# Moving two weight splits from the smallest to the largest attention tiles, and cutting the key-compression rows in two

## What is computed

```python
h = x @ w_in_even[li]
qa, ka, va, qn, kc, vc, ksl, vsl, kw, vw, g = _split(h, EVEN_SPLITS)
o_a = diff_attention(qa, ka, va, diff_lambda[li], diff_subln[li], layer)      # 4 heads x 2 halves, causal
# nsa_attention: 8 query heads in 2 groups, three branches
blocks = t[:, cmp_idx] + pe[j]          # windows of 32 rows of kc and vc, every 16 rows
hid    = gelu(blocks @ w1[j] + b1[j]);  out = hid @ w2[j]                     # 31 compressed keys and values
o_c = softmax(q . kc) vc;  o_s = softmax(q . rope(ksl)) vsl;  o_w = softmax(q . rope(kw)) vw
o_b = g0 * o_c + g1 * o_s + g2 * o_w
mix = concat(o_a, o_b) @ w_out_even[li]
x = layer_norm(ALPHA * x + mix); ...
```

## Time and profile before

| | |
|---|---|
| median of 3 runs | 2456.62 us (2455.29 to 2457.24) |
| the profiled execution | 2456.84 us, span 2455.5 us |
| mean granted TensorE clock | 0.959 |
| busy share of the span | TensorE 93%, VectorE 42%, ScalarE 29%, GpSimd 4% |

### The profile page before, as it was taken

The page is one execution under the profiler, slowest core; times in us unless marked ns, Lnnn a source line. Parts: engine busy times, 40 slices in busy tenths (PEclk is TensorE's granted clock), DMA queues, the critical chain, the costliest instruction groups (busy, mean ns, idle before and its releaser), DMA issues.

```text
span 2455.5 us, 28478 instructions
## 1 busy us (share of the span) xinstructions
PE 2286.5 (93%) x11871; PEld 1686.7 (69%) x11871; DVE 1043.5 (42%) x1904; ACT 703.8 (29%) x1188; POOL 95.4 (4%) x96
## 2 busy tenths in 40 slices
PE   7998899979989999899788989999999999899998
PEld 6866687864434343587555778888787777788887
DVE  5347465342322233434566534233521455342335
ACT  4324354310100010223345223133223362231331
POOL 2001001010000000000000000000000000000000
PEclk9989899989999999999889999999989999999999
DMA  5232242359999999522100222323132201223230
GB/s 194 86 127 82 78 163 105 102 223 392 427 426 427 426 428 427 203 81 69 69 1 1 90 100 103 103 86 103 36 132 86 86 2 39 100 102 103 86 103 34
DMA packets 106740, 370.34 MB, mean 151 GB/s; under 512 B 15040, under 2 KB 20672, under 8 KB 94320
## 3 DMA queue, kind: packets, MB, share of 16 engines
q1 hardware_dynamic: 103584, 361.65, 39.1%
q0 software_dynamic: 3024, 6.83, 0.9%
HBM read 368.38 MB, written 4.19 MB: 152 GB/s over the span
## 4 chain that ended last, share of the span: by engine, by line
PE 78%; DMA 10%; DVE 8%; ACT 2%; issue 1%; POOL 1%; SPq 0%; DVEq 0%; ACTq 0%; POOLq 0%
PE PB L450 52%; PE PB L1898 8%; PE PB L467 5%; PE PB L460 4%; PE PB L769 4%; DMA Z<-in_w_exp_gate 4%; PE PB L661 3%; DMA FL_raw<-in_w_exp_gate 1%; DMA FH_raw<-in_w_exp_gate 1%; DMA Z<-in_w_exp_down 1%; PE PB L785 1%; DVE W L442 1%; DMA FL_raw<-in_w_exp_down 1%; PE PB L666 1%; ACT W L434 1%
## 5 line engine op out<-in xcount | busy, mean ns | idle before, releaser
L442 DVE TENSOR_TENSOR W<-R,W 128x2048 fp32r<-128x2048 f32 (+1 forms) x128 | 291.4, 2277 | 663.1 <-ACT W L434 663.0
L450 PE MATMUL PB<-W,FH 128*128 128x512 f32 (+1 forms) x1792 | 558.4, 394 | 8.1 <-DVE FL L823 6.7
L434 ACT ACTIVATE W<-R 128x2048 fp32r<-128x2048 f32 (+1 forms) x128 | 243.5, 1903 | 678.8 <-PE PB L450 671.7
L450 PEld LDWEIGHTS PB<-W,FH 128*128 128x128 f32 x1792 | 332.4, 190 | 77.4 <-DVE FL L823 8.1
L450 PE MATMUL PB<-W,hid 128*128 128x512 f32 x1536 | 349.6, 389 | 1.0 <-DVE X L2923 1.0
L450 PE MATMUL PB<-W,FL 128*128 128x512 f32 (+1 forms) x896 | 348.8, 389 | 0.0
L450 PE MATMUL PB<-FH,W 128*128 128x512 f32 (+1 forms) x1152 | 327.4, 369 | 15.6 <-ACT nsp L2878 14.3
L450 PEld LDWEIGHTS PB<-W,hid 128*128 128x128 f32 x1536 | 288.1, 188 | 61.0 <-DVE X L2923 1.4
L450 PEld LDWEIGHTS PB<-FH,W 128*128 128x128 f32 x1152 | 210.7, 191 | 52.1 <-ACT nsp L2878 14.7
L450 PE MATMUL PB<-FL,W 128*128 128x512 f32 (+1 forms) x576 | 212.2, 368 | 0.0
L450 PEld LDWEIGHTS PB<-W,FL 128*128 128x128 f32 x896 | 169.7, 189 | 35.4
(11 more groups left out here) (329 smaller groups left out, 2643.8 us busy)
## 6 DMA issues: line engine op xcount, KB each, us to landing
R<-in_mlp_w_up SPq DMA_DIRECT2D x32, 1024.0 KB, 5.3
R<-in_mlp_w_down SPq DMA_DIRECT2D x32, 1024.0 KB, 5.0
Z<-in_w_exp_down SPq DMA_DIRECT2D x14, 2048.0 KB, 30.6
Z<-in_w_exp_up SPq DMA_DIRECT2D x13, 2048.0 KB, 36.4
R<-in_w_exp_gate SPq DMA_DIRECT2D x11, 2048.0 KB, 32.3
W_raw<-in_w_exp_up SPq DMA_DIRECT2D x10, 2048.0 KB, 31.3
R<-in_w_exp_up SPq DMA_DIRECT2D x9, 2048.0 KB, 30.9
R<-in_w_in SPq DMA_DIRECT2D x12, 1024.0 KB, 5.4
```

The costliest lines, as they stand in the source:

```text
L434: k.A.e.activation(w.splits[w.split_of[u]][0][:, 0:m], w.rows(u), ACT.Copy).then_inc(*w.hi.tick(u))
L442: k.V.e.tensor_tensor(wl[:, 0:m], w.rows(u), wh[:, 0:m].bitcast(F32), ALU.subtract).then_inc(*w.lo.tick(u))
L450: ins = te.matmul(bank, l, r, start=(start and n == 0), stop=(stop and n == len(terms) - 1), skip_group_check=True)
```

## The change

Three edits. The two `cut` steps move from around `nsa[1, 1]` to the middles of `nsa[3, 0]` and `nsa[3, 1]`. The `windows` step becomes two, one for each of keys and values, with a pair between them. The copies into partitions 64 to 127 of `cs` go from VectorE to ScalarE (`act_fours`), with a bank of the transposes kept until the doubling of `ksl`, and VectorE's doubling made to wait for ScalarE's copies.

```diff
-    return ([("ks", 3)] + d3[0:2] + [("five", 0), ("five", 1), d3[2], ("five", 2), ("five", 3), d3[3], ("windows",), d2[0],
-             ("hidden", 0), d2[1], ("hidden", 1), d2[2], ("hidden", 2), d2[3], ("hidden", 3), ("dn", 3), d1[0], d1[1],
+    return ([("ks", 3)] + d3[0:2] + [("five", 0), ("five", 1), d3[2], ("five", 2), ("five", 3), d3[3], ("windows", 0), d2[0],
+             ("windows", 1), ("hidden", 0), d2[1], ("hidden", 1), d2[2], ("hidden", 2), d2[3], ("hidden", 3), ("dn", 3), d1[0], d1[1],
              ("biased",), d1[2], ("small",), d1[3], ("kc",), d0[0], d0[1], ("dn", 2), d0[2], d0[3], ("few", 3)]
-            + nsa[3, 0] + [("dn", 1), ("few", 2)] + nsa[3, 1] + [("dn", 0)] + nsa[2, 0] + [("few", 1)] + nsa[2, 1]
-            + nsa[1, 0] + [("few", 0), ("cut", 0)] + nsa[1, 1] + [("cut", 1)] + nsa[0, 0] + nsa[0, 1]
+            + nsa[3, 0][0:2] + [("cut", 0)] + nsa[3, 0][2:] + [("dn", 1), ("few", 2)] + nsa[3, 1][0:2] + [("cut", 1)]
+            + nsa[3, 1][2:] + [("dn", 0)] + nsa[2, 0] + [("few", 1)] + nsa[2, 1] + nsa[1, 0] + [("few", 0)] + nsa[1, 1]
+            + nsa[0, 0] + nsa[0, 1]
             + [("out", 0), ("out", 1), ("out", 2)])
...
     def fours(i):
-        pe_doubled(k, "four", i, k.dve_step.at("four", i), Banks.FLIPS)
+        pe_doubled(k, "four", i, k.kk_doubled.at("ks", i), Banks.FLIPS)
...
-        T.wait_ge(*k.dve_step.at("windows"))
+        T.wait_ge(*k.dve_step.at("windows", 1))
...
             elif p == 5:
+                act_fours(k, i)
                 if i:
                     act_doubled(k, "ks", i - 1)
...
+def act_fours(k, i):
+
+    k.A.wait_ge(*k.kk_turned.at("four", i))
+    b4 = k.banks["four", i][:].rearrange("p (j g t) -> p j g t", j=2, g=2)
+    lo = 128 * i - 1 if i else 0
+    for j in range(2):
+        ins = k.A.e.activation(k.cs[64:128, j, :, lo:128 * i + 127], b4[64:128, j, :, (0 if i else 1):128], ACT.Copy)
+    ins.then_inc(*k.act_step.tick("four", i))
...
-    lo = 128 * i - 1 if i else 0
     for j in range(2):
-        ve.tensor_copy(k.cs[0:64, j, :, 128 * i:128 * i + 128], b4[0:64, j])
-        ins = ve.tensor_copy(k.cs[64:128, j, :, lo:128 * i + 127], b4[64:128, j, :, (0 if i else 1):128])
+        ins = ve.tensor_copy(k.cs[0:64, j, :, 128 * i:128 * i + 128], b4[0:64, j])
     ins.then_inc(*k.dve_step.tick("four", i))
...
+    V.wait_ge(*k.act_step.at("four", i))
     twice(k, k.double["ks"][i], rows[:, 256:384]).then_inc(*k.kk_doubled.tick("ks", i))
...
-def dve_windows(k):
+def dve_windows(k, j):
 
     k.V.wait_ge(*k.projected.at("even", 5, 3))
     k.V.wait_ge(*k.dve_step.at("four", 3))
-    for j in range(2):
-        for g in range(2):
+    k.V.wait_ge(*k.act_step.at("four", 3))
+    for g in range(2):
...
```

More of the change, by code:

```diff
@@ L2614, in dve_fives @@
     twice(k, k.double["kw"][i], rows[:, 0:128]).then_inc(*k.kk_doubled.tick("kw", i))
-def dve_windows(k):
+def dve_windows(k, j):
     k.V.wait_ge(*k.projected.at("even", 5, 3))
     k.V.wait_ge(*k.dve_step.at("four", 3))
-    for j in range(2):
-        for g in range(2):
[L2623 to L2628, removed]
+    k.V.wait_ge(*k.act_step.at("four", 3))
+    for g in range(2):
+        for h in range(2):
+            src = k.cs[:, j, g, 16 * h:16 * h + 512].rearrange("p (n c) -> p c n", c=16)[:, 0:16:2, :]
+            dst = k.windows[j][:, 512 * h:512 * h + 512].rearrange("p (l c) -> p l c", l=8)[:, :, 32 * g:32 * g + 32]
+            ins = k.V.e.tensor_tensor(dst, src, k.pe[:, j, 8 * h:8 * h + 8].unsqueeze(2).to_broadcast([P, 8, 32]),
+                                      ALU.add)
+    ins.then_inc(*k.dve_step.tick("windows", j))
 def dve_hidden_turned(k):
@@ L2727, in dve_even_attention @@
             elif kind == "windows" and what == "score":
-                dve_windows(k)
+                dve_windows(k, i)
             elif kind == "biased" and what == "score":
```

## The result

| | before | after |
|---|---|---|
| median | 2456.62 us (5 runs, 2454.28 to 2459.13) | 2441.31 us (5 runs, 2438.08 to 2446.31) |
| the profiled execution, its span | 2456.84, 2455.5 us | 2444.77, 2443.5 us |
| mean granted clock | 0.959 | 0.963 |

The ratio is 0.9942 (0.9927 to 0.9958): faster by 15.3 us between the medians, by 12.1 between the profiled executions. The forecast was 12.9. The number came out near, its parts did not: the tail gave more than was forecast, and a wait that no part named took about 7 us of it back, in another layer.

The account below looks back on a forecast made before the run. TensorE held 78% of the chain, so gains could come only where it waits or runs at the lower clock. The terms -12.5 + 4.3 - 1.2 - 3.5 = -12.9 us took 2456.8 to 2444 us, range 2435 to 2452.5.

Parts of the forecast that it names:

- Tail: End of the even layer's attention, which the splits leave: TensorE's idles and the half clock after them shrink, -12.5 us.
- Rival B: Small tiles in the tail stay at half clock, so the tail gives 7.5 us: 2449 us; chance 0.22.
- Splits in nsa[3,*]: Third and seventh pair of the biggest tiles, where the splits go: costs of 1.8 and 2.5 us, +4.3 us.
- Copies: Compression rows: two of four copies per tile go from VectorE to ScalarE, shortening the round to 2.65 us; -1.2 us.
- Windows: Window additions split into two steps, so the next tiles' reductions come earlier and TensorE idles less; -3.5 us.
- Nothing else: Rest of the program: SyncE's and GpSimd's orders stay the same, and semaphore edits cost nothing that a row shows.
- rival D: Longer gaps before the third pair's applies drop the clock through the biggest tiles; slower, up to 2506 us; chance 0.03.
- Rival C: Splits only moved: new places cost 8.4 us, the tail gives 6.6; -2.9 in all, 2454 us; chance 0.12.

Follow-up runs that it names:

- e6: The kernel before with only half of the copies moved to ScalarE, windows in one part and splits in the tail; ratio 0.9982.
- e1: The change plus one line that sets the PSUM bank turn to 856 before the odd layer's attention; ratio 0.9926, median 2435.99 us.
- e3: The kernel before with only the two splits moved between the largest tiles, odd layer's bank turn held at 856; ratio 0.9955.
- e10: The change with the bank turn at 856 and VectorE's half of both splits three steps behind ScalarE's half; ratio 0.9918.
- e11: The change with the bank turn at 856, VectorE's half three steps behind ScalarE's for the first split, one step for the second; ratio 0.9922.
- e9: The change with the bank turn at 856 and the second split put back between nsa[1,1] and nsa[0,0]; ratio 0.9971.
- e7: The change with the bank turn at 856 and both splits moved among the smallest tiles of the first attention (d0); ratio 0.9942.
- e8: The change with the bank turn at 856 and both splits moved into nsa[2,0] and nsa[2,1]; ratio 0.9940.

## Why the prediction was right, and where it was not

The forecast, faster at 2444 us, held (2441.31), and the tail won for the reason given: the two idles closed, and the low clock behind them did not come. That the sum came out so near is luck, as the parts show.

- **Tail, -12.5 us: too small.** The "rest" of the table fell by 16.5 us against the profile before (15.5 against the mean of the five with both splits in the tail). The point at 1317.8 that the prediction counts from is a group of transposes, not of scores; from there to the output projection it is 39.1 us before and 22.6 after, where the prediction said 26. The step that failed is the density after the move, taken as 85% with 2.6 us of half clock kept. It is 95% (12.52 and 19.65 busy in 13.40 and 20.48 us) with no half clock: 9.4 us came from pauses (50.35 - 39.27 against 33.88 - 32.17) and 7.1 from the clock (39.27 against 32.17). The clock's part varies with the execution: it would be 4.3 against the profile of e6. That small tiles need more copies per matmul cost little: no wait of TensorE there is over 1 us. Rival B falls: the tiles of 128 columns run at 1.00 here, with no such pause before them.
- **Splits in nsa[3,*], +4.3: right, by a mix.** The first cost 3.1 (forecast 1.8), the second 0.8 (2.5), with the shorter nsa2: 3.9. In the first GpSimd's power is late, which the prediction did not have.
- **Copies, -1.2: too small.** 2.8. The round is 2.46 us, not 2.65 (doublings at 1153.86 and 1156.32), and the second doubling, behind the table load, ended 5.3 us after the pass's first transposes (1151.69 - 1146.35), not 5.5 (1152.9 - 1147.41): 0.5 us in all beside the forecast, so 1.7 in the pass of these two profiles and 1.9 by the means. No drain stands behind the load here either: it ends at 1150.42, the next activation starts at 1150.43. Another 0.9 us came in d3, whose low clock (in the kernel before from 1160.5) does not occur in any of the nine profiles with the copies.
- **Windows, -3.5: too large.** The walk was right: idles of 1.45 and 2.65 us, forecast 1.5 and 2.4, and d2 is 3.1 us shorter in these two profiles. By the means it is 2.1 (1.7 to 1.8 with the copies alike); the rest is a second low stretch that the profile before happened to have.
- **Nothing else: wrong.** "SyncE's and GpSimd's orders are the same; edits of semaphores cost nothing that a row shows" left out the banks. +6.8 to 7.4 us in "odd". The terms without it are -15.5 + 3.9 - 2.8 - 2.1 = -16.5, and e1 measures 0.9926, -18.2 us (14.7 to 21.8); with it they are about -9.7, and the change measures -14.2 (10.3 to 17.9 by its ratio) and -12.1 by the profiles. Why the change, by its ratio, gains more than these terms stays open. That 12.9 stood near the result is therefore luck, a cancellation: a tail and copies taken some 4.6 us too small, against windows taken 1.4 too large and a wait of about 7 that was not seen.
- One sum is off: in rival D, 18 - 12.9 is 5.1, not 4.9; nothing hangs on it.
- Rival C (the splits only moved) and D (clock falls in the biggest tiles) did not occur in the change. In e3, e10 and e11 the clock does fall within nsa3, as D has it, but for stretches of about 4 us each, not for the whole of it.

## What to carry to other kernels

A step that moves in one layer can move a resource counter that later layers use: compare the waits of the whole program, not of the place alone, and reset such a counter at a layer's start. In this kernel two dependent halves on two engines cost least where the second engine was behind anyway, so the busiest place was the cheapest; try such places as well as the idle ones. A pause in front of small tiles was paid twice here, the second time in clock (9.4 and 7.1 us).

## What the hardware showed

- GpSimd's power of 128x4 takes 1.01 us, and 2.98 us where VectorE's subtraction of two SBUF operands (2.28 us) ran when it started (the change, e1, e3 and e9; in the change it had begun 0.17 us before). It ended 0.87 us after the subtraction. With the subtraction moved (e10) it takes 1.01. The Trainium skill ("SBUF — State Buffer", Who interferes with whom) says that a VectorE instruction with two SBUF inputs and a GpSimd instruction that reads SBUF exclude each other, and the second waits until the first is done; these rows agree.
- ScalarE and VectorE read the same PSUM bank at the same time, in different partitions, at usual durations: 0.65 us for ScalarE's two copies of 64x256 and 0.75 for VectorE's two, at 1152.50 and 1152.44. In the tile before they ran apart, at 1150.64 and 1148.97, and took the same.
- The same code gets a stretch of low clock in one execution and not in another: d2 of e7 and e8 takes 23.8 us, all at 1.00, and 25.2 to 25.4 in the other kernels with divided windows, whose granted clock there is 0.93.
